# Two weight units started side by side at the head of two stages, squares added in pairs, and the seventh unit's split moved, in a one-core decoder step

## What is computed

```python
x = x + 0.5 * swiglu(rms(x))                 # FFN 1, hidden width 2752
h = rms(x); z = h @ w_in                     # projection: queries, keys, values, two gate blocks
oA = sparse attention (top-k keys per query); oB = block-sparse attention
x = x + (sigmoid(gA) * (oA @ w_up_a) + sigmoid(gB) * (oB @ w_up_b)) @ w_out
x = x + 0.5 * swiglu(rms(x))                 # FFN 2

def rms(x): return x * rsqrt(mean(x * x, axis=-1) + 1e-6) * g
```

## Time and profile before

| what | value |
|---|---|
| median of 3 runs | 656.43 (655.72 to 658.95) |
| the profiled execution: its own time | 658.87 |
| the profiled execution: span from first to last instruction | 657.2 |
| PE busy | 642.0 (98% of the span) |
| PE weight loads busy | 619.0 (94%) |
| DVE, ACT, POOL busy | 425.7, 299.7, 157.6 |
| mean granted clock of PE | 0.990 |
| DMA, mean | 157 GB/s |

### The profile page before, as it was taken

One profiled execution on the slowest core, in us unless ns is written; L12 is line 12 of the kernel. 1 busy time (PEld: TensorE's weight loads), 2 busy tenths in 40 slices (PEclk: granted clock), 3 DMA queues, 4 the chain that ended last, 5 costly groups with the idle time before them and its releaser, 6 DMA issues.

```text
span 657.2 us, 12957 instructions
## 1 busy us (share of the span) xinstructions
PE 642.0 (98%) x4798; PEld 619.0 (94%) x4798; DVE 425.7 (65%) x657; ACT 299.7 (46%) x489; POOL 157.6 (24%) x220
## 2 busy tenths in 40 slices
PE   8799999999999999998999999999999999999998
PEld 5799999999999999876889889999999999999998
DVE  6666565666555568899896855986666565665441
ACT  7534444344344434546543557645535344444330
POOL 1577775000011216446521210062000000000000
PEclk9799999999999999999997999999999999999999
DMA  8576766545555453422322222554354545446530
GB/s 329 203 223 214 242 207 221 161 150 172 182 165 165 161 189 126 141 88 87 105 98 65 98 97 77 179 196 161 129 169 152 184 145 183 157 147 209 157 123 19
DMA packets 31978, 103.05 MB, mean 157 GB/s; under 512 B 5120, under 2 KB 5824, under 8 KB 31936
## 3 DMA queue, kind: packets, MB, share of 16 engines
q1 hardware_dynamic: 27504, 96.22, 44.1%
q0 software_dynamic: 3616, 4.73, 2.6%
q10 hardware_dynamic: 816, 1.54, 0.6%
HBM read 100.77 MB, written 1.70 MB: 156 GB/s over the span
## 4 chain that ended last, share of the span: by engine, by line
PE 88%; DVE 5%; ACT 2%; issue 2%; POOL 1%; DMA 1%; ACTq 0%; SPq 0%; DVEq 0%; POOLq 0%
PE ps L1103 27%; PE ps L1105 27%; PE ps L1104 27%; DVE roots L1022 1%; DVE wlo L796 1%; DVE acc L960 1%; POOL act_tmp L474 1%; PE ps L1293 1%; DMA x<-in_x 1%; PE ps L1279 1%; PE ps L1216 1%; ACT whi L555 1%; PE ps L1248 1%; PE ps L1330 1%; PE ps L1125 0%
## 5 line engine op out<-in xcount | busy, mean ns | idle before, releaser
L796 DVE TENSOR_TENSOR wlo<-raw,whi 128x1024 fp32r<-128x1024 f32 (+1 forms) x181 | 228.6, 1267 | 121.3 <-ACT whi L555 121.1
L1103 PE MATMUL ps<-nhi,whi 128*128 128x288 f32 x952 | 288.6, 303 | 2.4 <-DVE nlo L822 2.4
L1104 PE MATMUL ps<-nlo,whi 128*128 128x288 f32 x952 | 282.4, 297 | 0.0
L1105 PE MATMUL ps<-nhi,wlo 128*128 128x288 f32 x952 | 281.4, 296 | 0.0
L555 ACT ACTIVATE whi<-raw 128x1024 fp32r<-128x1024 f32 (+1 forms) x181 | 182.4, 1030 | 138.6 <-PE ps L1105 130.7
L1103 PEld LDWEIGHTS ps<-nhi,whi 128*128 128x128 f32 x952 | 179.8, 189 | 7.6 <-issue 5.1
L1104 PEld LDWEIGHTS ps<-nlo,whi 128*128 128x128 f32 x952 | 180.0, 189 | 0.8
L1105 PEld LDWEIGHTS ps<-nhi,wlo 128*128 128x128 f32 x952 | 180.3, 189 | 0.0
L1103 PE MATMUL ps<-hhi,whi 128*128 128x288 f32 x336 | 99.5, 296 | 0.0
L1104 PE MATMUL ps<-hlo,whi 128*128 128x288 f32 x336 | 99.1, 295 | 0.0
L1105 PE MATMUL ps<-hhi,wlo 128*128 128x288 f32 x336 | 98.8, 294 | 0.0
(11 more groups left out here) (181 smaller groups left out, 706.8 us busy)
## 6 DMA issues: line engine op xcount, KB each, us to landing
raw<-in_weights SPq DMA_DIRECT2D x166, 512.0 KB, 3.4
raw<-in_weights SPq DMA_DIRECT2D x16, 384.0 KB, 3.6
kt<-in_cache_kidx_a POOLq DMA_DIRECT2D x32, 32.0 KB, 2.6
kt<-in_cache_k_b POOLq DMA_DIRECT2D x16, 64.0 KB, 3.4
kt<-in_cache_k_a POOLq DMA_DIRECT2D x32, 32.0 KB, 3.2
vb_pg<-in_cache_v_b POOLq DMA_DIRECT2D x16, 64.0 KB, 3.3
cst<-in_constants ACTq DMA_DIRECT2D x1, 980.0 KB, 8.1
x<-in_x SPq DMA_DIRECT2D x2, 288.0 KB, 4.0
```

Of the source, the lines that this page charges most:

```text
L796: nc.vector.tensor_tensor(wlo[:, v % NU, 0:nk, 0:w], raw[:, v % NR, 0:nk, 0:w], whi[:, v % NU, 0:nk, 0:w].bitcast(F32), ALU.subtract).then ...
L1103: nc.tensor.matmul(out[0:w, 0:N], h, hi, start=start and i == 0, stop=False)
L1104: nc.tensor.matmul(out[0:w, 0:N], h, lo, start=False, stop=False)
L1105: ins = nc.tensor.matmul(out[0:w, 0:N], l, hi, start=False, stop=stop and done is not False and i == len(ks) - 1)
```

## The change

- SP loads unit 1 in two halves too: its first half between the first two parts of x and the second half of unit 0, its second half behind the last part of x.
- ACT and DVE split the first half of unit 1 before the second half of unit 0.
- PE multiplies blocks 0 to 3 of unit 0, blocks 0 to 3 of unit 1, then blocks 4 to 7 of both (`two_units`).
- POOL adds the first norm's squares in four pairs, in place, without a chain; `mean_square(0)` adds the four sums in PSUM with four matmuls. It still stands behind unit 2.
- In the projection PE multiplies blocks 0 to 6 of the first two units, then does `mean_square(1)`, then block 7 of both.
- In pair 0 of both FFNs, ACT asks for the Sqrt table ahead of the splits of units 4 and 5, and ACT and DVE split unit 6 behind the root and the reciprocal, ahead of pair 0's products; pair 1 then splits unit 7 alone.

```diff
@@ -310,8 +310,8 @@
 
         raw_in = [sem(f"raw_in{i}") for i in range(NR)]
 
-        (first_in, consts_in, gains_in, ptab_in, pages_in, out_done) = [sem(s) for s in
-            "first_in consts_in gains_in ptab_in pages_in out_done".split()]
+        (first_in, second_in, consts_in, gains_in, ptab_in, pages_in, out_done) = [sem(s) for s in
+            "first_in second_in consts_in gains_in ptab_in pages_in out_done".split()]
 
         x_in = [sem(f"x_in{i}") for i in range(len(X_PARTS))]
 
@@ -356,6 +356,7 @@
         FIRST_HALF = KB // 2
         PAGE_DMAS = 16 * 7 * N_SEQ * NPG
         MS_AFTER = (2, 1)
+        SQUARES = (KB // 2, KB // 2 + 1, KB // 2 + 2)
         MS_BANK = (7, 0, 7)
         BANKS_FREE = 3
         DOWN_FREE = 3
@@ -419,9 +420,13 @@
                     sp.dma_start(raw[:, 0, half, :], src[:, half, :]).then_inc(first_in, 16)
                     load_x(0)
                     load_x(1)
+                    sp.dma_start(raw[:, 1, half, :], a["weights"][1][:, half, :]).then_inc(second_in, 16)
                     half = slice(FIRST_HALF, KB)
                     sp.dma_start(raw[:, 0, half, :], src[:, half, :]).then_inc(raw_in[0], 16)
                     load_x(2)
+                elif v == 1:
+                    half = slice(FIRST_HALF, KB)
+                    sp.dma_start(raw[:, 1, half, :], src[:, half, :]).then_inc(raw_in[1], 16)
                 else:
                     sp.dma_start(raw[:, v % NR, 0:nk, :], src[:, 0:nk, :]).then_inc(raw_in[v % NR], 16)
 
@@ -467,13 +472,9 @@
                         ins.then_inc(*((pool_chain, 1) if k < KB else (squares_ready, 1)))
                 pool_ops[0] += 2 * KB - 2
 
-            for k in range(1, KB):
-                pool.wait_ge(x_squared, k + 1)
-                if k >= 2:
-                    pool.wait_ge(pool_chain, k - 1)
-                ins = nc.gpsimd.tensor_tensor(ssq, sq[:, 0, :] if k == 1 else ssq, sq[:, k, :], ALU.add)
-                ins.then_inc(*((pool_chain, 1) if k < KB - 1 else (squares_ready, 1)))
-            pool_ops[0] = KB - 2
+            for k in range(0, KB, 2):
+                pool.wait_ge(x_squared, k + 2)
+                nc.gpsimd.tensor_tensor(sq[:, k, :], sq[:, k, :], sq[:, k + 1, :], ALU.add).then_inc(squares_ready, 1)
             nc.gpsimd.dma_start(ptab[:], a["page_table"].rearrange("a b -> (a b)")[None, :]).then_inc(ptab_in, 16)
             pool.wait_ge(ptab_in, 16)
             n_pool = a["cache_v_a"].shape[0]
@@ -557,10 +558,7 @@
 
             def first_split_hi(v, half):
 
-                if v or half:
-                    act.wait_ge(raw_in[v], 16)
-                else:
-                    act.wait_ge(first_in, 16)
+                act.wait_ge(raw_in[v] if half else (first_in, second_in)[v], 16)
                 ks = slice(half * FIRST_HALF, (half + 1) * FIRST_HALF)
                 nc.scalar.activation(whi[:, v, ks, :], raw[:, v, ks, :], ACT.Copy).then_inc(w_hi if half else first_hi, 1)
 
@@ -598,11 +596,11 @@
             act.wait_ge(gains_in, 16)
             for k in range(KB):
                 norm_hi(0, k)
-                if k == 3:
+                if k == FIRST_HALF - 1:
+                    first_split_hi(1, 0)
                     first_split_hi(0, 1)
             act.dma_start(cst[:], a["constants"]).then_inc(consts_in, 16)
-            for half in range(2):
-                first_split_hi(1, half)
+            first_split_hi(1, 1)
             for v in (2, 3):
                 split_hi(v)
                 for k in range(4 * (v - 2), 4 * (v - 1)):
@@ -614,18 +612,20 @@
                 gp = (f - 1) * FB + p
                 w = P if p < FB - 1 else FTAIL
                 if p == 0:
+                    preload(ACT.Sqrt)
                     split_hi(v - 1 + AHEAD)
                     split_hi(v + AHEAD)
-                    preload(ACT.Sqrt)
                     root(0 if f == 1 else 2)
                     preload(ACT.Silu)
+                    split_hi(v + 1 + AHEAD)
                 if p == FB - 2:
                     split_hi(v - 1 + AHEAD)
                     split_hi(v + AHEAD)
                 act.wait_ge(gate_scaled, gp + 1 + LOOP_PAIRS * it)
                 nc.scalar.activation(act_tmp[0:w, p % 2, 0, :], act_tmp[0:w, p % 2, 0, :], ACT.Silu).then_inc(silu_done, 1)
                 if p not in (0, FB - 2):
-                    split_hi(v - 1 + AHEAD, it)
+                    if p > 1:
+                        split_hi(v - 1 + AHEAD, it)
                     if p < FB - 1:
                         split_hi(v + AHEAD, it)
                 act.wait_ge(prod_ready, gp + 1 + LOOP_PAIRS * it)
@@ -829,10 +829,10 @@
             first_split_lo(0, 0)
             for k in range(KB):
                 norm_lo(0, k)
-                if k == 3:
+                if k == FIRST_HALF - 1:
+                    first_split_lo(1, 0)
                     first_split_lo(0, 1)
-            for half in range(2):
-                first_split_lo(1, half)
+            first_split_lo(1, 1)
             for v in (2, 3):
                 split_lo(v)
             dve.wait_ge(consts_in, 16)
@@ -850,6 +850,7 @@
                     split_lo(v - 1 + AHEAD)
                     split_lo(v + AHEAD)
                     inverse_rms(0 if f == 1 else 2)
+                    split_lo(v + 1 + AHEAD)
                 if p == FB - 2:
                     split_lo(v - 1 + AHEAD)
                     split_lo(v + AHEAD)
@@ -861,7 +862,7 @@
                     dve.wait_ge(h_lo, gp - 1 + LOOP_PAIRS * it)
                 nc.vector.tensor_tensor(tmp[0:w, p % 2, 0, :], up_bank[up, 0:N], rstd[up, :],
                                         ALU.mult).then_inc(pair_free, 1)
-                if p not in (0, FB - 2):
+                if p not in (0, 1, FB - 2):
                     split_lo(v - 1 + AHEAD, it)
                 dve.wait_ge(silu_done, gp + 1 + LOOP_PAIRS * it)
                 dve.wait_ge(pair_free, gp + 1 + BANKS_FREE + LOOP_PAIRS * it)
@@ -1121,15 +1122,30 @@
             def mean_square(r):
                 if r == 0:
                     pe.wait_ge(consts_in, 16)
-                pe.wait_ge(squares_ready, r + 1)
-                nc.tensor.matmul(ps[MS_BANK[r]][:, 0:N], c_(C_ONE, P), ssq, start=True, stop=True).then_inc(ms_done, 1)
+                pe.wait_ge(squares_ready, SQUARES[r])
+                sums = [sq[:, k, :] for k in range(0, KB, 2)] if r == 0 else [ssq]
+                for i, s in enumerate(sums):
+                    ins = nc.tensor.matmul(ps[MS_BANK[r]][:, 0:N], c_(C_ONE, P), s, start=i == 0, stop=i == len(sums) - 1)
+                ins.then_inc(ms_done, 1)
 
             normed = lambda k: (nhi[:, k, :], nlo[:, k, :], P)
+
+            def two_units(v, outs, cut, x_base, between=None):
+
+                for g in range(2):
+                    unit(v + g, outs[g], normed, kl=range(cut), done=False, x_sem=n_lo, x_base=x_base)
+                if between is not None:
+                    mean_square(between)
+                for g in range(2):
+                    unit(v + g, outs[g], normed, kl=range(cut, KB), start=False, x_sem=n_lo, x_base=x_base)
 
             def pair(f, p, it=0, r=None):
 
                 v = first[f"G{f}"] + 2 * p
                 pe.wait_ge(pair_free, (f - 1) * FB + p + 1 + LOOP_PAIRS * it)
+                if r == 0:
+                    two_units(v, ps[0:2], FIRST_HALF, 0)
+                    return
                 for g in range(2):
 
                     if r is not None and g == 0:
@@ -1311,9 +1327,10 @@
                         ins.then_inc(tok_T, 1)
                 if u >= 4:
                     pe.wait_ge(z_ready, last_of_bank(u) + 1)
-                unit(vp + u, ps[z_bank(u)], normed, x_sem=n_lo if u == 0 else None, x_base=KB)
                 if u == 0:
-                    mean_square(1)
+                    two_units(vp, (ps[z_bank(0)], ps[z_bank(1)]), KB - 1, KB, between=1)
+                elif u > 1:
+                    unit(vp + u, ps[z_bank(u)], normed)
                 if u - 1 in NORMED:
                     i = index_among(u - 1, NORMED)
                     pe.wait_ge(zsq_ready, i + 1)
```

## The result

| | before | after |
|---|---|---|
| median of 7 runs each | 656.43 (655.62 to 659.44) | 652.60 (650.84 to 654.46) |
| the profiled execution: its own time | 658.87 | 652.55 |
| its span; mean granted clock | 657.2; 0.990 | 650.5; 0.995 |
| time around the span | 1.67 | 2.05 |

The ratio after to before is 0.9929 with a 95% interval of 0.9906 to 0.9953: 0.7% faster, 3.1 to 6.2 us. The medians lie 3.8 us apart, the two profiled executions 6.3. The forecast was 649.5, 6.9 us under the median, in a range of 647.9 to 653.2. So the range held the result, but some three of the seven microseconds did not arrive in the median, although they are in the profile. Where they went is what the experiments are for.

The account below looks back on a forecast made before the run. PE, busy 98%, was taken as the bound, losing time to its stop for POOL's sum of squares and the half clock behind it. Head 5.7 plus projection 1.2 is 6.9 us off 656.43: 649.5, range 647.9 to 653.2.

Parts of the forecast that it names:

- the 5.7 of the sum: At the head, unit 4 begins at 23.25 instead of 28.96, a gain of 5.7 us.
- the earlier end of unit 2: At the head, unit 2 ends at 17.2 instead of 18.25, counted as 1.05 us of the 5.7.
- a start at 17.95: First mean square's start with POOL's sums laid out against DVE's splits; 18.25 by a mere median; 18.0 was taken.
- The projection: Seven blocks of unit 1 fill PE's idle time ahead of the last block of x: 1.2 us, ends 0 and 1.4.
- PE wants none of it before the fourth unit behind, ten us on: In the projection, DVE's first evictions come 2.2 us later, at no cost to PE.
- the first rival: DVE becomes the bound in the projection and its gain is lost: 650.7 us, chance 0.10.
- a new wait of PE for DVE in that stretch: Sign of being wrong: new waits of PE for DVE between 231 and 265, in the projection.
- The seventh unit and the second FFN: nothing: The seventh unit's earlier split and the moved table load, in both FFNs, gain and cost nothing; first product about 24.5.
- the step from the profile to the median: For the whole kernel, 6.9 us off the profiled 658.87 gives 652.0; against the median 656.43, 649.5 was forecast.
- the second, four sums of 1.6 each: Rival at the head: pair sums always come second to a split, PE stops until 19.85; gain 5.05, 651.4 us, chance 0.12.
- the third, constants too late: Rival at the head: late constants hold PE, clock falls; 656.9 us (no change), chance 0.06, or 659.8 (slower), chance 0.03.
- a stop of 1.4 us is safe: At the head, a PE stop of 1.4 us did not lower the clock, so a 0.8 us stop keeps 2.4 GHz.

Follow-up runs that it names:

- chain-sum kernel: The changed kernel with POOL's sum of squares as before (chain of seven, one matmul), the rest kept: 657.73 us, ratio to before 0.9993.
- units in turn: The changed kernel with loads, splits and products of units 0 and 1 in the order of before, pair sums kept: 653.65 us, ratio 0.9941.
- The two versions with root and reciprocal ahead of the split: Changed kernel with mean square behind unit 3, units 6 and 7 split early, projection's root and reciprocal early; one sum (649.83 us) or two sums (650.70 us).
- the two more of before: Two more profiled executions of the kernel before, unchanged: both spans 654.2 us at a granted clock of 0.995.
- no seventh unit: The changed kernel with the seventh unit's split and the Sqrt table load where they were before: 651.83 us.
- both kernels of one sum: Changed kernel with POOL's tree to one sum, mean square behind unit 3: 650.54 us; the same with reordered splits, early root and reciprocal: 649.83 us.
- the changed kernel again: The changed kernel, unchanged, run again beside the kernel before: 651.87 us, ratio 0.9914.
- projection in turn: The changed kernel with the projection's first two units in turn and the mean square behind the first, as before: 653.4 us, ratio 0.9947.
- PE kept busy: The kernel before with 20 matmuls of ones between unit 2 and the first mean square: 656.37 us against 658.90, ratio 0.9964.
- the three that go on from it: Changed kernel with POOL's tree and mean square behind unit 3: one sum 650.54 us; plus reordered splits, early root and reciprocal 649.83; that with two sums 650.70.

## Why the prediction held, and what it missed

**The bound and the mechanism were right.** The sum of squares on POOL bounded the head, it ended where it was laid out (17.77 for 17.8), PE's stop came down to 0.44 us between records, the clock stayed up, and unit 4 gained 5.84 us for the 5.7 of the sum. The chain-sum kernel shows that the pair sums are the part that carries this. The sum books 1.05 of its 5.7 to "the earlier end of unit 2"; in the kernel of units in turn unit 2 ends 0.7 us later than in after and the down projection at the same time, within what a profile can tell, so that share is not the side by side start's.

**Sums and splits.** The prediction weighed a start at 17.95, with each sum laid out against DVE's splits, against 18.25 by the median; the 17.91 is the former's. The Trainium skill's page "SBUF — State Buffer", section "Who interferes with whom", on which it draws there, has the later of two such instructions wait for the earlier one. The trace agrees: the two sums that started within a split took 1.17 and 1.42 us and ended 0.65 and 0.67 behind its end, the two others took 0.81 and 0.79, and the split that started within a sum took 1.47 for the 1.23 of the one before.

**The projection was right by luck in part.** It was put at 1.2, with ends of 0 and 1.4, and the trace gives 0.88, out of two errors that cancel in part. The two units side by side brought 1.46: the mean square in between took 0.49 (from 222.88 to 223.37, 0.133 ahead of the second matmul behind it), where the prediction has 0.7. The step that failed is the one that puts DVE's later evictions at nothing, "PE wants none of it before the fourth unit behind, ten us on": ten us on, at the second swap matmul, DVE had not caught up, and that took 0.58. It is the first rival in part, and one of the signs that the prediction itself gave for being wrong, a new wait of PE for DVE in that stretch. The two versions with root and reciprocal ahead of the split get the 0.58 back.

**The seventh unit and the second FFN: nothing,** as forecast, by the kernel without them and by the 261.7 us. The first products come at 24.34 (forecast 24.5). POOL's page loads start 2.85 us earlier (25.35 for 28.20) and not 4.6, which changed nothing.

**What failed is the step from the profile to the median:** "Its time lies 2.4 above the median of the three runs, 656.43; against that I forecast" 649.5. The 658.87 was an execution of before with the stretch at half clock near 352. A time of 656.43 is a span of some 654.8, in the table's group at 0.992: 0.6 above the two profiles without that stretch and 2.4 below the two with it. The profiled after had that stretch in full, at 346 to 354, and its way from the last swap matmul to the attention's output takes the same 74.3 us, so the two profiles differ by the change alone, 6.3 in time and 6.7 in span. The runs differ by the change and by how often and how long the clock falls later. Over the 76 executions of before the mean span is 655.8 at a mean clock of 0.9916; over thirteen of after it is 650.4 at 0.9949. That is 5.4 of the profiles' 6.7 us, so some 1.3 are missing, and later falls are the only loss for which the profiles show a cause; with 0.4 us more around the span the mean times, 657.44 and 652.46, lie 5.0 apart. Counting lost clock instead gives the same as a rough estimate: before lost 5.5 us of clock on average, 3.4 of them in the head if its fall was in every execution, so 2.1 later; after lost 3.3, all of it later. The medians show 3.8 or 7.1, as the runs of before fall.

**Open.** Why the clock falls later more often after than before isn't settled: no execution was made in which only the attention's start moved. The fourteen profiles show where it falls. Twelve have a fall that begins between 344 and 354, all but the two more of before. Four, all of kernels without the long stop (no seventh unit, both kernels of one sum, the changed kernel again), have one at 282 to 288 as well, behind a wait of PE of 1.4 us for ACT that stands in all fourteen; one, units in turn, has one at 293. In the four the earlier fall costs no time and the later one is shorter: from the down projection's end to the last swap matmul it is 94.5 us in the changed kernel with and without it, and from there to the attention's output 72.7 with it, against 74.3. In the eight kernels without the long stop (the changed one, units in turn, projection in turn, no seventh unit, PE kept busy, and the three that go on from it) 6 of 66 executions kept a clock of 1.00 throughout; none of before's 76 did. Nor is it known what the 0.4 us around the span are: 2.05 in the four kernels with pair sums, 1.65 in those with a chain or a tree. By the rivals: the second, four sums of 1.6 each, and the third, constants too late, did not happen. Two ends of the prediction's ranges don't come out of its terms (the own range begins at 648.7 by 6.3 and 1.4, the range given at 648.0); neither bears on the result.

## What to carry to other kernels

Where PE is almost always busy, look for the stop that lowers its clock, and count the slow stretch behind it with the stop: here a wait of 4.2 us and the slow stretch behind it gave 5.8 together. Work put in front of PE's wait only helps if the thing waited for comes earlier too; find the chain behind it first. When an engine off the path is made later, follow its queue to the place where the path next needs it. And before a median is forecast from a profile, ask which of the times of the kernel the profile is of, and whether what sets them apart is in the stage that is changed.

## What the runs showed of the hardware that was not expected

The clock fell while PE was recorded as busy without a stop from 318 on: at 352 in the profile of before, in 32-column matmuls, as shown above. It also fell behind stops that were shorter than the head's. In the second profile of the changed kernel, PE waits 1.4 us for ACT and is then recorded as busy (a timeline row, and windows as above):

```profile
281.26 0.64 PE L1216 MATMUL ps<-kt,qz 128*32 128x256 f32 x8 [1.43 <-ACT probs L683]
...
282.00:288.00 6.00, 6.00 (x37) 0.72 0.29 90
347.00:352.00 5.00, 5.00 (x29) 0.66 0.28 108
```

The first profile of the same kernel has the same wait, and the clock stays:

```profile
281.20 0.64 PE L1216 MATMUL ps<-kt,qz 128*32 128x256 f32 x8 [1.43 <-ACT probs L683]
...
282.00:288.00 6.00, 6.00 (x47) 1.00 0.30 90
```

At the start, a wait of 1.9 us for x in the kernel with PE kept busy was followed by a fall at 11 to 15, where the wait of 1.4 us at the same place had not been in the profile of before. The prediction's inference that a stop of 1.4 us is safe held at the head and is not a rule.
